# Half-unit pieces: attention and recurrence products placed twice per dense unit instead of once

## The reference, cut to what matters

```python
def mixer(z, w_in, gla_w2, gla_b2, gla_gn, q_norm, k_norm, w_pa, w_pb, b_merge, w_out, cos, sin):
    h = z @ w_in
    (q_a, k_a, v_a, r_a, lr_f, lr_b, q_b, k_b, v_b, g_a, g_b) = jnp.split(h, SPLIT_POINTS, axis=-1)
    a = gla_branch(q_a, k_a, v_a, r_a, lr_f, lr_b, gla_w2, gla_b2, gla_gn)
    b = attention_branch(q_b, k_b, v_b, q_norm, k_norm, cos, sin)
    y = (jax.nn.sigmoid(g_a + b_merge[0]) * (a @ w_pa)
         + jax.nn.sigmoid(g_b + b_merge[1]) * (b @ w_pb))
    return y @ w_out
```

## Time and profile before

| | |
|---|---|
| median of 3 runs (range) | 2104.45 us (2096.8 to 2106.95) |
| profiled execution: its own time | 2102.54 us |
| profiled execution: span | 2101.2 us |
| PE busy | 96% |
| DVE, ACT busy | 68%, 48% |
| mean granted TensorE clock | 0.979 |
| mixer of layer 0 (about 233 to 500 us) | clock 0.94 |
| mixer of layer 1 (about 919 to 1170 us) | clock 0.99 |

### The profile page before, as it was taken

How to read it: one execution, slowest core, us unless ns; L and a number is a source line. 1 busy time by engine, 2 the same in 40 slices (tenths; PEclk the granted TensorE clock), 3 DMA queues, 4 the chain that set the end, 5 groups by cost and what they waited for, 6 DMA issues and landing times.

```text
span 2101.2 us, 37146 instructions
## 1 busy us (share of the span) xinstructions
PE 2018.6 (96%) x15561; PEld 1913.5 (91%) x15561; DVE 1438.4 (68%) x2409; ACT 1009.0 (48%) x1628; POOL 39.2 (2%) x56
## 2 busy tenths in 40 slices
PE   6999999999999999999999999989999998999998
PEld 6999888789999999988889999978899997889998
DVE  5777554358776677655558877676698666679964
ACT  5444444355444444445555544345655444565532
POOL 0000000000000000000000000030000003000000
PEclk9999999899999999999999999999999999999999
DMA  6675322235675477532224676333445553344553
GB/s 237 245 279 200 120 101 66 76 111 202 249 275 206 164 262 261 203 138 101 81 92 166 247 285 252 135 106 112 172 152 201 190 170 122 112 159 161 201 181 121
DMA packets 51247, 363.24 MB, mean 173 GB/s; under 512 B 6566, under 2 KB 8006, under 8 KB 9224
## 3 DMA queue, kind: packets, MB, share of 16 engines
q1 hardware_dynamic: 51080, 360.86, 48.8%
HBM read 359.78 MB, written 1.05 MB: 172 GB/s over the span
## 4 chain that ended last, share of the span: by engine, by line
PE 84%; DVE 8%; ACT 4%; issue 3%; DMA 0%; SPq 0%; DVEq 0%; ACTq 0%
PE bank L405 23%; PE bank L406 23%; PE bank L407 23%; PE bank L604 1%; PE bank L678 1%; DVE full L1487 1%; DVE w_lo L1445 1%; ACT w_hi L996 1%; PE bank L437 1%; PE bank L441 1%; PE bank L692 1%; PE bank L438 1%; PE bank L555 1%; PE bank L497 1%; PE bank L649 1%
## 5 line engine op out<-in xcount | busy, mean ns | idle before, releaser
L405 PE MATMUL bank<-xn_hi,w_hi 128*128 128x256 f32 (+1 forms) x2480 | 725.3, 292 | 20.9 <-DVE w_lo L1445 20.9
L407 PE MATMUL bank<-xn_lo,w_hi 128*128 128x256 f32 (+1 forms) x2480 | 713.2, 288 | 0.0
L406 PE MATMUL bank<-xn_hi,w_lo 128*128 128x256 f32 (+1 forms) x2480 | 713.1, 288 | 0.0
L405 PEld LDWEIGHTS bank<-xn_hi,w_hi 128*128 128x128 f32 x2480 | 474.2, 191 | 40.3 <-issue 38.5
L407 PEld LDWEIGHTS bank<-xn_lo,w_hi 128*128 128x128 f32 x2480 | 474.3, 191 | 0.1
L406 PEld LDWEIGHTS bank<-xn_hi,w_lo 128*128 128x128 f32 x2480 | 473.4, 191 | 0.9
L1445 DVE TENSOR_TENSOR w_lo<-raw_b,w_hi 128x1024 fp32r<-128x1024 f32 (+2 forms) x282 | 357.5, 1272 | 130.4 <-ACT w_hi L996 128.9
L1445 DVE TENSOR_TENSOR w_lo<-raw_a,w_hi 128x1024 fp32r<-128x1024 f32 (+1 forms) x280 | 351.6, 1261 | 138.1 <-ACT w_hi L996 136.9
L996 ACT ACTIVATE w_hi<-raw_b 128x1024 fp32r<-128x1024 f32 (+2 forms) x282 | 306.9, 1092 | 220.7 <-PE bank L407 186.2
L996 ACT ACTIVATE w_hi<-raw_a 128x1024 fp32r<-128x1024 f32 (+1 forms) x280 | 302.1, 1083 | 220.7 <-PE bank L407 188.6
L405 PE MATMUL bank<-h_hi,w_hi 128*128 128x272 f32 (+1 forms) x704 | 202.0, 287 | 0.0
(11 more groups left out here) (324 smaller groups left out, 3179.2 us busy)
## 6 DMA issues: line engine op xcount, KB each, us to landing
raw_b<-in_weights SPq DMA_DIRECT2D x123, 1024.0 KB, 4.8
raw_a<-in_weights SPq DMA_DIRECT2D x121, 1024.0 KB, 4.8
ada_raw<-in_ada_w SPq DMA_DIRECT2D x48, 1024.0 KB, 4.9
raw_a<-in_weights SPq DMA_DIRECT2D x16, 1408.0 KB, 5.7
raw_b<-in_weights SPq DMA_DIRECT2D x16, 1408.0 KB, 5.7
raw_b<-in_weights SPq DMA_DIRECT2D x2, 1152.0 KB, 5.9
raw_a<-in_weights SPq DMA_DIRECT2D x2, 640.0 KB, 4.2
cst<-in_const SPq DMA_DIRECT2D x1, 1152.0 KB, 9.3
```

The lines of the kernel that those rows point to most:

```text
L405: pe.matmul(o, wh, xh, start=start, stop=False)
L406: pe.matmul(o, wl, xh, start=False, stop=False)
L407: return pe.matmul(o, wh, xl, start=False, stop=stop)
```

## The change: what it does

tile, half_tiles, values_part and token_tiles get a call-back, `between`, in the middle of a unit, and mixer passes one that steps the chains. So PE steps each chain twice for each unit from 4 to 41, in the middle and at the end. The chains get further yields, so that what was one piece becomes two and the number of units a chain takes stays the same. ACT and DVE are still stepped once for each unit. The order of the two directions in a head's masked product is turned round (1, then 0), and the sum of squares of head h-1 moves into the first piece of head h. ACT waits for the end-gate product by its own mark. Pieces that now stand in the middle of a unit: 555 for bank 2, 623, g = 0 of 632 and 633, 659, the first transposes of the meta tokens, 609, 585 of direction 0, 604 for the first two token tiles, 678 and 681, and the log gates 543.

```diff
@@ tile, and likewise half_tiles, values_part and token_tiles
+            if between is not None and kk == k_tiles // 2 - 1:
+                between()
@@ gla, PE
-                for b, col in ((2, C_CUM[d]), (3, C_END[d])):
+                for b, col, name in ((2, C_CUM[d], "cum"), (3, C_END[d], "end")):
                     take(b)
                     for t, (c0, n) in enumerate(TILES):
                         m = pe.matmul(bank[b][:, c0:c0 + n], c.la[0:n, t, d * 256 + p * P:d * 256 + p * P + P],
                                       cst[0:n, col:col + n], start=True, stop=True)
-                m.then_inc(*k.up("gla_mm", ("cum", l, i)))
+                    m.then_inc(*k.up("gla_mm", (name, l, i)))
+                    yield
                 yield
                 pe.wait_ge(*k.at("gla_v", ("kend", l, i)))
...
                 m.then_inc(*k.up("gla_mm", ("turn", l, i)))
+                yield
                 yield
...
+            if h:
+                norm_of(h - 1)
+            yield
+            for d in (1, 0):
                 i, b = 2 * d + p, 2 + d
                 take(b)
...
                 free[b] = [("gla_v", ("att", l, h, d))]
-            yield
-            pe.wait_ge(*k.at("gla_v", ("att", l, h, 1)))
+                yield
+            yield
+            pe.wait_ge(*k.at("gla_v", ("att", l, h, 0)))
...
+                if t == 1:
+                    yield
             m.then_inc(*k.up("gla_mm", ("o", l, h)))
             yield
@@ attention, PE
                 free[b_t] = [("att_v", ("turned", l, j - 2))]
+                yield
             elif j == 6:
...
+                    if g == 0:
+                        yield
+            else:
+                yield
             if 0 < j < 6:
...
             free[b_s] = [("att_a", ("exp", l, 0))]
+            yield
             yield
             turn(0, 0)
...
                     free[b_o] = [("x_lo", ("b", l, p))]
+            yield
             if 0 < i <= len(tiles):
                 turn(i, tiles[i - 1][2] - 1)
@@ mixer, PE
+            def between(u=u):
+                step(chains, u)
...
-                tile(u0 + u, b, TA if u == 12 else live, c.xn_hi, c.xn_lo)
+                tile(u0 + u, b, TA if u == 12 else live, c.xn_hi, c.xn_lo, between=between)
@@ gla, ACT
+            act.wait_ge(*k.at("gla_mm", ("end", l, i)))
             act.wait_ge(*k.at("gla_v", ("kinv", l, i)))
...
         for h in range(GLA_H):
             yield
+            yield
             act.wait_ge(*k.at("gla_mm", ("o", l, h)))
...
             act.activation(c.a_hi[:, h, live], c.full[:, 0, live], ACT.Copy).then_inc(*k.up("x_hi", ("a", l, h)))
-            yield
@@ gla, DVE
-            for d in range(2):
+            for d in (1, 0):
...
-            yield
+                yield
             yield
...
             low(c.a_lo[:, h, live], f, c.a_hi[:, h, live], ("a", l, h))
-            yield
```

More of the change, by code:

```diff
@@ L415, in end_unit, with tile @@
         assert k.count["unit_done"] == u + 1
-    def tile(u, b, cols, xh, xl, k_tiles=KD, rows=P, step=P):
+    def tile(u, b, cols, xh, xl, k_tiles=KD, rows=P, step=P, between=None):
         take(b)
@@ L464, in leading_units, with half_tiles @@
         tiles_as_ready(u + 2, 2, to, c.xn_hi, c.xn_lo, stage)
-    def half_tiles(u, bs, cols, xh, xl, ready=()):
+    def half_tiles(u, bs, cols, xh, xl, ready=(), between=None):
         for b in bs:
@@ L476, in half_tiles @@
                 m = product(bank[b][:, cols], wh[:, s], wl[:, s], xh[:, kk, cols], xl[:, kk, cols], kk == 0, kk == 3)
+            if between is not None and j == 0:
+                between()
         end_unit(u, m)
@@ L578, in gla, with norm_of @@
                 yield
+        def norm_of(h):
+            pe.wait_ge(*k.at("gla_a", ("square", l, h)))
+            take(2)
+            pe.matmul(bank[2][:, LIVE[l]], c.ones, c.sq[:, LIVE[l]], start=True, stop=True).then_inc(*k.up("gla_mm", ("sum", l, h)))
+            free[2] = [("gla_a", ("root", l, h))]
         for h in range(GLA_H):
             p, hr = h // 2, slice(64 * (h % 2), 64 * (h % 2) + 64)
-            for d in range(2):
+            if h:
+                norm_of(h - 1)
+            yield
+            for d in (1, 0):
                 i, b = 2 * d + p, 2 + d
@@ L604, in gla @@
                     m = pe.matmul(o, lh, rh, start=q == 0, stop=q == len(todo) - 1, skip_group_check=True)
+                if t == 1:
+                    yield
             m.then_inc(*k.up("gla_mm", ("o", l, h)))
             yield
[L607 to L610, removed]
-            yield
+        norm_of(GLA_H - 1)
         free[4] = [("gla_v", ("normed", l, GLA_H - 1))]
@@ L695, in attention, with values_part @@
             yield
-    def values_part(u, j):
+    def values_part(u, j, between):
         wh, wl = weights(u)
@@ L708, in values_part, with token_tiles @@
                 m = pe.matmul(bank[b][0:n, :], c.xn_lo[:, kk, cs], wh[:, s], start=False, stop=kk == KD - 1)
+            if t == 1:
+                between()
         end_unit(u, m)
-    def token_tiles(u, b):
+    def token_tiles(u, b, between):
         take(b)
@@ L731, in mixer @@
             elif u < 8:
-                values_part(u0 + u, u - 4)
+                values_part(u0 + u, u - 4, between)
                 if u == 7:
@@ L735, in mixer @@
             elif u == 13:
-                token_tiles(u0 + u, 1)
+                token_tiles(u0 + u, 1, between)
                 free[1] = [("tile_a", ("vb", l))]
@@ L748, in mixer @@
                 xh, xl = (c.b_hi, c.b_lo) if branch_b else (c.a_hi, c.a_lo)
-                half_tiles(u0 + u, bs, live, xh, xl, ready)
+                half_tiles(u0 + u, bs, live, xh, xl, ready, between)
                 for b in bs:
```

## The result

| | before | after |
|---|---|---|
| median (range) of 5 runs each | 2104.45 us (2093.8 to 2106.95) | 2116.24 us (2111.19 to 2116.31) |
| ratio, 95% interval | | 1.008 [1.0056, 1.0104] |
| profiled execution: its own time, clock | 2102.54 us, 0.979 | 2111.19 us, 0.983 |
| mixer 0, first product to first product of the output projection | 239.2 us | 244.4 us |
| mixer 1, the same | 210.9 us | 220.5 us |

That is within the range of 2098 to 2122 and 4 us above the forecast, but it is beyond the 0.5% to which I had given most of the chance.

A forecast was written before the change was run, and what follows sets the result against it. PE, busy 96% of the span, was taken to bound the kernel. Waits 10.6 + passages 6.4 - clock 13.1 + clock lost anew 5 = +8.9 us; forecast 2112.0 us, 8-in-10 range 2098 to 2122.

The forecast's parts named there:

- Waits (10.6): Both mixers: PE asks for results half a unit sooner while producers hardly start sooner; 10.6 us lost, bounds 4 and 15.
- passages (6.4): Units cut in the middle: one more passage from dense to chain and back, 0.15 us each, 6.4 us lost.
- Duplicated keys: Unit 14: moving g = 0 into mid-unit does not hide the key wait, as DVE makes states first; 1.1 us lost per layer.
- The extra mark I cost at nothing: End gates: ACT's added wait costs nothing, because they are done while DVE makes the decayed keys.
- steady part: Head units: masked product no longer covers DVE whole; 0.3 us in unit 18, layer 0, about 0.5 and 0.9 over further units.
- Pieces move half a unit earlier: All moved pieces in the mixers: no product added or removed, each only stands half a unit, 1.6 us, sooner.
- A sign of being wrong that the prediction named: Mixers: the clock falls in the middle of the split clusters all the same.
- 13.1, the most that the change can win back: Layer 0, four stretches of long fp32 clusters: low clock costs 13.1 us, counted as won back by splitting.
- Clock lost anew 5: New idle stretches behind unit 14 and in unit 16, and remaining clusters, pull the clock down; 5 us, between 0 and 13.
- Rival 2: Both mixers: idle stretches pull the clock down as often as long clusters did; +17.0 us, 2120 us, chance 0.17.
- my own case: Whole kernel: waits and passages outweigh the net clock gain; +8.9 us, 2107 to 2117 us, chance 0.40.
- Rivals 1 and 3: First: clock won back whole, small waits, 2098 us, chance 0.22; third: waits half hidden by slow stretches, 2105 us, chance 0.21.

The follow-up runs named there:

- e12_nowait: Changed kernel with units 10, 16 and 18 uncut and, in unit 14, DVE's first key rotation ahead of the states; 2100.0 us, 1.0001 of the kernel before.
- e1_late: Changed kernel with pieces in mid-unit only from unit 19 on, earlier ones behind their units; 2100.8 us, 1.0009 of the kernel before.
- e2_early: Changed kernel with pieces in mid-unit only up to unit 18, later ones behind their units; 2108.8 us, 1.0045 of the kernel before.
- e11_clusters: Changed kernel cut only in units 4, 20, 23, 26 and 29 of each layer, the long clusters; 2090.3 us, 0.9958 of the kernel before.
- e4_dve: Changed kernel with DVE taking unit 14's first key rotation ahead of the states, the second behind them; 2107.0 us, 1.0044 of the kernel before.
- e5_act: Changed kernel with ACT's recurrence step ahead of its copy of the unit in units 9, 12 and 15; 2106.8 us, 1.0034 of the kernel before.
- e8_none: Changed kernel with no unit cut; reversed directions, moved sum of squares and ACT's mark stay; 2099.5 us, 1.0006 of the kernel before.

## Why the prediction was right in size and wrong in the clock

**Waits (10.6) and passages (6.4): right.** The sum of 17.0 was measured as 17.1 at equal clock. That it fits to 0.1 us is luck: the waits came out 1.4 higher and the passages 1.3 lower. Within it: PE's waits in mixer 0 add up to 8.8 us (before 1.7) and in mixer 1 to 8.5 (before 3.6), so 12.0 us are new, and 17.1 - 12.0 = 5.1 is left for 43 cuts, 0.12 each; e12_nowait gives 0.12 for 39 (counted in its trace). I had 10.6 and 0.15. The cost per cut is what remains after the waits, and it is not one number: e1_late gives 0.14, e2_early 0.22, e11_clusters next to nothing.
- Duplicated keys +1.1 and +1.0 (I had 1.1 each), by the mechanism named: e4_dve. Meta-token probabilities 2.1, output behind silu 1.5, rotation in unit 10 0.8 and 0.9, all as worked out; ACT's start behind its copy is a part of the cause by e5_act; the rest is the end-gate product. "The extra mark I cost at nothing" holds only as long as ACT starts late. The later rotations together came to 0.8 where I had 2.0, and late probabilities in mixer 1 to 1.1 more than before, where I had 0.9 for its steady part.
- Missed: waits of 2.6 us at the end of mixer 0, for which I had 0.8 with the steady part: 0.6 ahead of unit 34, which takes the bank that ACT copies unit 33 out of, 1.3 ahead of units 36 and 37, whose banks DVE frees when it has multiplied them with the gates, and 0.7 ahead of an output (line 699). With the last output in the middle of unit 33, its 2.1 us no longer stand between units 33 and 34 and cover ACT and DVE. e8_none, with the same pieces behind the unit, has none of these waits. Mixer 1 of before had two of them already (1.3 and 0.6 us for line 405, the cover being absent there), and the prediction passed them over when it wrote that only the keys make a wait above 0.3.
- "Pieces move half a unit earlier" was too general. In a recurrence head the masked product of direction 0 moves from behind its unit into the middle of the next, and the output (604) from behind unit 19 + 3h into and behind unit 20 + 3h, so these stand later. It cost nothing by itself (e8_none).

**The clock (-13.1 + 5): the step that failed, in both terms.** What is measured is -1.3 instead of -8.1. A sign of being wrong that the prediction named came true: the clock fell in the middle of a split cluster (unit 23), with dense products 0.23 apart behind it, and mixer 0 stood at 0.96, not above.
- "13.1, the most that the change can win back" was read from one execution at 0.979, 0.0023 or 4.3 us below the mean of before. e11_clusters, which differs from e8_none (clock 0.9808) by nothing but the cuts in these clusters, wins 8.5 us against before. The mechanism was right, the term was mis-sized: 8.5 instead of 13.1.
- "Clock lost anew 5" was too small: against e11_clusters the full change gives back 0.0039, 7.2 us. Without its long waits, and with three units left uncut in each mixer, 4.4 of them are back (e12_nowait), and e5_act's shorter waits brought as much. That long waits are the cause isn't shown by this: e4_dve removed the longest and its clock rose by half as much, e2_early keeps all those of units 10 to 18 and its clock is no lower than that of before, and e1_late has none of the new waits of units 10 to 18 and still lies 0.0018 (3.4 us) below e11_clusters. Of the last 2.8 us only the place is seen, the two-thirds clusters among half units; that their surroundings are the cause is not shown either. So what pulls the clock down again in the full change stays open.

So the medians came close to the forecast partly by luck: the loss was forecast 6.8 us too small, and I started from a low-clock execution of before, 3.7 us above the mean, which hid more than half of that. Rival 2 (+17.0, the clock not won back) described what happened better than my own case; its time of 2120 was 4 us too high because the 2102.54 was a low-clock execution. Rivals 1 and 3 needed small or hidden waits, and the waits came in full.

The Trainium skill, TensorE: Matmul & The Clock Gate, section "Why this matters for your kernels", ties a drop of throughput in mid-kernel to idle gaps between bursts. The gaps that it means are longer than any wait of these mixers (2.8 us at most), so no run here tests it. It isn't the whole: e11_clusters won 0.0046 by breaking stretches in which PE was busy throughout, without removing a wait.

## What to carry to other kernels

Spread small products only where they make a long cluster: cuts in five units of each mixer gave here the whole gain of the clock (8.5 us) for some 0.1 to 0.3 us, and cuts in every unit cost 17.1 us in waits and passages and kept 1.3 us of that gain. Leaving whole units of dense work around the pieces fits these runs; that it is what keeps the gain is not shown. Before a piece on PE is moved earlier, work out for each producer what it does first (its copy of the unit, another chain's step), since PE's position alone changes nothing there; and look whether the piece covered a wait where it stood, as the last output did. And split every time into work and clock over many runs before a difference of a per cent is explained: one profile's falls of the clock are a draw.

## What was not expected of the hardware

- The time of one and the same program on one core ranges over 18.6 us (0.9%) with the granted clock, from 0.986 to 0.977. The same page of the Trainium skill, section "What's actually happening", says that the slow stretch at a kernel's start differs from run to run; the runs here show the like in mid-kernel: the places of the falls differ between two executions of the changed kernel.
- A 7.2 us cluster of small fp32 products ran at full clock in one execution, and one cut to two thirds (line 699 took 2.48 us in it instead of 1.65) fell to half clock in another.
- Fifty small products between dense ones cost 0.31 us each, 0.15 for the product and the rest for the passages, and left the mean clock where it was.
- Cuts in five clusters of each mixer raised the mean clock from 0.9813 (85 runs) to 0.9859 (9 runs), though PE had been busy throughout those clusters and no wait was removed.
